# The last expert's down projection by quarters of the output columns, and the third norm's transposes by token block

## The reference

```
# 16 experts, cap = 64 tokens each, hidden width 2048
xe  = h[top_idx]                                   # (16, 64, 1024)
hid = silu(xe @ w_gate) * (xe @ w_up)              # (16, 64, 2048)
ye  = (hid @ w_down) * top_w                       # (16, 64, 1024)
x   = x + gate2 * zeros(512, 1024).at[top_idx].add(ye)
# second block
xn  = x * rsqrt(mean(x*x) + 1e-6) * g_mix          # the third norm of the kernel
z   = xn @ w_in_2 + b_in_2                         # first dense layer behind it
```

## Time and profile before

| | |
|---|---|
| median of 3 runs | 2202.88 us |
| the runs | 2198.74, 2203.45, 2202.88 us |
| the profiled execution, its own time | 2200.71 us |
| span of its records | 2198.9 us |
| mean granted clock of TensorE in it | 0.973 of full |
| PE, DVE, ACT, POOL busy | 91%, 27%, 19%, 1% of the span |
| HBM read, mean rate | 510.00 MB, 233 GB/s |

### The profile page before, as it was taken

How to read it: one execution, slowest core, us unless ns; L and a number is a source line. 1 busy time by engine, 2 the same in 40 slices (tenths; PEclk the granted TensorE clock), 3 DMA queues, 4 the chain that set the end, 5 groups by cost and what they waited for, 6 DMA issues and landing times.

```text
span 2198.9 us, 19559 instructions
## 1 busy us (share of the span) xinstructions
PE 1996.3 (91%) x8422; PEld 1112.1 (51%) x8422; DVE 602.6 (27%) x865; ACT 410.5 (19%) x617; POOL 28.3 (1%) x41
## 2 busy tenths in 40 slices
PE   3998999899968988888998889888879999999998
PEld 2555465444744434334343434343334477888887
DVE  4153437341141111010101011100126813322333
ACT  2135545500011000000000001000020213222222
POOL 0000000000000000000000000000030000000000
PEclk9999999999988999999999999999989999999999
DMA  9210033354426999999999999999972013333220
GB/s 341 77 39 20 6 110 115 120 179 141 172 96 262 415 416 416 417 417 417 415 416 416 415 416 416 416 416 417 417 254 77 20 39 115 96 96 97 96 75 39
DMA packets 143787, 513.37 MB, mean 233 GB/s; under 512 B 7891, under 2 KB 70355, under 8 KB 107731
## 3 DMA queue, kind: packets, MB, share of 16 engines
q1 hardware_dynamic: 141632, 503.35, 58.7%
q10 hardware_dynamic: 2070, 8.78, 1.0%
HBM read 510.00 MB, written 2.10 MB: 233 GB/s over the span
## 4 chain that ended last, share of the span: by engine, by line
PE 72%; DMA 18%; DVE 5%; ACT 4%; issue 1%; SPq 1%; ACTq 0%; DVEq 0%
PE ps L424 14%; DMA work<-in_w_exp_up 13%; PE ps L940 11%; PE ps L904 7%; PE ps L429 6%; PE ps L1083 5%; DMA ring<-in_w_exp_up 4%; PE ps L1042 4%; PE ps L1043 4%; PE ps L1044 4%; PE ps L862 3%; PE ps L642 3%; DMA ring<-in_ada_w 1%; PE ps L885 1%; PE ps L587 1%; PE ps L988 1%
## 5 line engine op out<-in xcount | busy, mean ns | idle before, releaser
L904 PE MATMUL ps<-work 128*64 128x512 f32 x1256 | 351.8, 595 | 41.7 <-DMA work<-in_w_exp_up 41.7
L424 PE MATMUL ps<-work,ring 128*128 128x512 f32 x784 | 345.9, 599 | 0.8 <-DVE work L1636 0.8
L904 PE MATMUL ps<-ring,work 128*64 128x512 f32 x792 | 242.8, 595 | 23.5 <-DMA ring<-in_w_exp_up 23.5
L424 PEld LDWEIGHTS ps<-work,ring 128*128 128x128 f32 x784 | 148.7, 192 | 186.7 <-issue 184.9
L904 PEld LDWEIGHTS ps<-work 128*64 128x64 f32 x1256 | 116.5, 137 | 232.4 <-issue 153.2
L1806 DVE TENSOR_TENSOR work<-work,ps 64x512 f32<-64x512 f32 x64 | 42.0, 692 | 505.1 <-ACT work L1358 504.5
L1358 ACT ACTIVATE work<-ps 64x512 f32<-64x512 f32 x64 | 32.6, 584 | 758.3 <-PE ps L904 758.3
L429 PE MATMUL ps<-ring,work 128*128 128x256 f32 x640 | 143.0, 386 | 2.5 <-DVE work L1703 1.7
L904 PEld LDWEIGHTS ps<-ring,work 128*64 128x64 f32 x792 | 80.8, 137 | 126.5 <-issue 82.4
L940 PE MATMUL ps<-work 128*64 128x512 f32 x600 | 140.6, 620 | 3.7 <-issue 3.1
L1042 PE MATMUL ps<-xh,wh 128*128 128x512 f32 x352 | 137.0, 389 | 0.0
(11 more groups left out here) (239 smaller groups left out, 1859.5 us busy)
## 6 DMA issues: line engine op xcount, KB each, us to landing
work<-in_w_exp_gate SPq DMA_DIRECT2D x80, 1024.0 KB, 23.2
work<-in_w_exp_up SPq DMA_DIRECT2D x77, 1024.0 KB, 23.5
work<-in_w_exp_down SPq DMA_DIRECT2D x75, 1024.0 KB, 20.9
ring<-in_w_exp_down SPq DMA_DIRECT2D x53, 1024.0 KB, 21.0
ring<-in_w_exp_up SPq DMA_DIRECT2D x51, 1024.0 KB, 22.4
ring<-in_w_exp_gate SPq DMA_DIRECT2D x48, 1024.0 KB, 22.5
ring<-in_w_in SPq DMA_DIRECT2D x27, 1024.0 KB, 5.5
ring<-in_ada_w SPq DMA_DIRECT2D x24, 1024.0 KB, 6.4
```

The lines of the kernel that those rows point to most:

```text
L424: i = e.matmul(bank(bk), piece(key)[:, off + k, 128 * j:128 * j + 128], rhs(k), start=(k == 0), stop=(k == (last or nk) - 1))
L904: i = e.matmul(PS[64 * gu:64 * gu + 64, fb, :], at(XET + 128 * k + 64 * z, 64), flat(key)[:, 512 * fb:512 * fb + 512], start=(k == 0), sto ...
```

## The change

Only the last expert is treated differently, and what follows it.

- The pieces of its down weights are cut another way. Piece n = 2q + half holds 256 output columns (quarter q) and 1024 rows of the hidden width (one half), as eight blocks of 128 rows: its rows in memory are 1 KB long where they were 4 KB.
- Down of the last expert is `last_down`: for each quarter q, 16 matmuls of 256 columns with a 128x64 stationary operand, all into partitions 64 to 127 of bank 4 or 5 (alternating by quarter). Each quarter is complete after two pieces.
- After the first half of quarter q, PE does `combine_quarter(q - 1)`: four matmuls of 256 columns with a 128x128 stationary operand into banks 6 and 7, with the two-deep wait as before, now on `x_fa`. The last quarter is combined behind all.
- DVE multiplies each quarter by the gate (64x256) and adds four 128x256 blocks to `X` (`add_quarter`). In the last quarter the additions are interleaved with the norm's reciprocals and scalings: addition tc+1 stands ahead of the scaling of block tc.
- ACT squares columns 0 to 767 of each token block once quarter 2 is added, adds the epsilon, and squares only the last 256 columns of a block after its last addition; the square root takes the rest as its bias.
- The transposes of the third norm go by token block for the first four feature blocks, which fill four banks; the other four feature blocks go as before.
- GpSimd waits for the two memsets behind the transposes where it waited for the last addition.

```
+def last_down():
+    e.wait_ge(s["x_hc"], 4 * NE)
+    e.wait_ge(s["x_xa"], 2 * NE)
+    for n in range(8):
+        q, half = n // 2, n % 2
+        key = ("ed", NE - 1, n)
+        e.wait_ge(*got[key])
+        if half == 0:
+            e.wait_ge(s["x_ym"], (30, 30, 31, 32)[q])
+        for k in range(8):
+            i = e.matmul(PS[64:128, 4 + q % 2, 0:256], at(HIDT + 64 * (8 * half + k), 64),
+                         piece(key, 8)[:, k, :], start=(half + k == 0), stop=(half + k == 8))
+        i.then_inc(s["x_dn"], 1)
+        if half == 0 and q > 0:
+            combine_quarter(q - 1)
+    combine_quarter(3)
+def combine_quarter(q):
+    ...
+    for tc in range(TC):
+        m = 4 * q + tc
+        if m < 2:  e.wait_ge(s["x_hc"], 4 * NE - 1 + m)
+        else:      e.wait_ge(s["x_fa"], m - 1)
+        e.matmul(bank(6 + m % 2, 256), at(OHWT + 128 * tc, 128), at(YE + 256 * q, 256),
+                 start=True, stop=True).then_inc(s["x_fb"], 1)
# PE, third norm
-turn(XS3, [0, 1, 2, 3], lambda c: normed(3, c), t3_free, s["t_pe"])
+for c in range(TC):
+    e.wait_ge(*normed(3, c))
+    for k in range(4):
+        ...
+        i = e.transpose(bank(k, 128, 128 * c), at(XS3 + 1024 * c + 128 * k, 128), ident)
+        if c == TC - 1:
+            i.then_inc(s["t_pe"], 1)
+for k in range(4, KD):
+    ...
# ACT
-rms(X, TP, st3, range(4), lambda c: None, s["r_a"])
+for c in range(TC):
+    e.wait_ge(s["x_fa"], 9 + c)
+    own(e.activation(..., at(X + 1024 * c, 768), ACT.Square, scale=1.0 / 32, accum_out=at(st3 + c, 1)))
+own(e.activation(at(st3a, 4), at(st3, 4), ACT.Identity, bias=cst("eps6")))
+for c in range(TC):
+    e.wait_ge(s["x_fa"], 13 + c)
+    own(e.activation(..., at(X + 1024 * c + 768, 256), ACT.Square, scale=1.0 / 32, accum_out=at(st3b + c, 1)))
+    e.activation(at(st3 + 4 + c, 1), at(st3b + c, 1), ACT.Sqrt, bias=at(st3a + c, 1)).then_inc(s["r_a"], 1)
# DVE
+for q in range(4):
+    e.wait_ge(s["x_dn"], 8 * (NE - 1) + 2 * q + 2)
+    e.tensor_tensor(rows(64, 128, YE + 256 * q, 256), PS[64:128, 4 + q % 2, 0:256],
+                    rows(64, 128, GATE2 + 256 * q, 256), ALU.mult).then_inc(s["x_ym"], 1)
+    if q < 3:
+        for tc in range(TC):
+            add_quarter(q, tc)
+add_quarter(3, 0)
+for c in range(TC):
+    if c + 1 < TC:
+        add_quarter(3, c + 1)
+    rms(3, X, XS3, st3, (c,), lambda c: e.wait_ge(s["x_fa"], 13 + c))
# GpSimd
-e.wait_ge(s["x_ca"], 64)
+e.wait_ge(s["pads"], 2)
```

More of the change, by code:

```diff
@@ L178 @@
     "wo_pe wo_t wo_x rt_pe rt_e rt_d "
-    "x_g x_oh x_xa x_xd x_ow x_ot x_oc x_gu x_sl x_hd x_ht x_hc x_dn x_ym x_cb x_ca "
+    "x_g x_oh x_xa x_xd x_ow x_ot x_oc x_gu x_sl x_hd x_ht x_hc x_dn x_ym x_cb x_ca x_fb x_fa "
     "pads dg i2_pe gl_sg gl_u cv_pe cv_a cv_d pw_in pw_o po_pe po_y mu_pe dv sqv vr_pe ln_a y_d y_a "
@@ L255, in build @@
         st1, st2, st3, st4, fin = small(8), small(8), small(8), small(8), small(8)
+        st3a, st3b = small(4), small(4)
         sh1, sc1, sh2, sc2 = small(8), small(8), small(8), small(8)
@@ L311, in source @@
                 return t["w_exp_gate" if kind == "eg" else "w_exp_up"][key[1], key[2] * 128:(key[2] + 1) * 128, :]
+            if kind == "ed" and key[1] == NE - 1:
+                q, half = key[2] // 2, key[2] % 2
+                return t["w_exp_down"][key[1], half * 1024:half * 1024 + 1024, q * 256:q * 256 + 256].rearrange("(k p) n -> p k n", p=128)
             if kind == "ed":
@@ L325, in rooms_of @@
                 return flat(key)
-            if kind == "ed" or (kind == "ff" and key[1] >= 22):
+            if (kind == "ed" and key[1] < NE - 1) or (kind == "ff" and key[1] >= 22):
                 return piece(key, 2)
@@ L885, in combine @@
                         e.matmul(bank(6 + dh), at(OHWT + 128 * tc, 128), at(YE + 512 * dh, 512), start=True, stop=True).then_inc(s["x_cb"], 1)
+            def combine_quarter(q):
+                if q == 0:
+                    e.wait_ge(s["x_oc"], NE // 2)
+                e.wait_ge(s["x_ym"], 31 + q)
+                for tc in range(TC):
+                    m = 4 * q + tc
+                    if m < 2:
+                        e.wait_ge(s["x_hc"], 4 * NE - 1 + m)
+                    else:
+                        e.wait_ge(s["x_fa"], m - 1)
+                    e.matmul(bank(6 + m % 2, 256), at(OHWT + 128 * tc, 128), at(YE + 256 * q, 256), start=True, stop=True).then_inc(s["x_fb"], 1)
+            def last_down():
[8 more added lines that the diff above has]
+                    for k in range(8):
+                        i = e.matmul(PS[64:128, 4 + q % 2, 0:256], at(HIDT + 64 * (8 * half + k), 64), piece(key, 8)[:, k, :],
+                                     start=(half + k == 0), stop=(half + k == 8))
+                    i.then_inc(s["x_dn"], 1)
+                    if half == 0 and q > 0:
+                        combine_quarter(q - 1)
+                combine_quarter(3)
             gather(0)
@@ L930, in _ @@
                     i.then_inc(s["x_ht"], 1)
+                if ex == NE - 1:
+                    last_down()
+                    break
                 for n in range(8):
@@ L942, in _ @@
                     i.then_inc(s["x_dn"], 1)
-            combine(NE // 2 - 1)
             def t3_free(k):
@@ L950, in t3_free @@
                     e.wait_ge(*turned_k(3, k - 4))
-            turn(XS3, [0, 1, 2, 3], lambda c: normed(3, c), t3_free, s["t_pe"])
+            for c in range(TC):
+                e.wait_ge(*normed(3, c))
+                for k in range(4):
+                    if c == 0:
+                        t3_free(k)
+                    i = e.transpose(bank(k, 128, 128 * c), at(XS3 + 1024 * c + 128 * k, 128), ident)
+                    if c == TC - 1:
+                        i.then_inc(s["t_pe"], 1)
+            for k in range(4, KD):
+                t3_free(k)
+                for c in range(TC):
+                    i = e.transpose(bank(k - 4, 128, 128 * c), at(XS3 + 1024 * c + 128 * k, 128), ident)
+                i.then_inc(s["t_pe"], 1)
             def xn_ready(k):
@@ L984, in _ @@
             e.wait_ge(s["pads"], 1)
-            e.wait_ge(s["x_ca"], 63)
+            e.wait_ge(s["x_fa"], 15)
             for k in range(31):
@@ L991, in _ @@
             pool_dense(9, 2, 5)
-            e.wait_ge(s["x_ym"], 32)
+            e.wait_ge(s["x_ym"], 33)
             for i in (3, 2, 0, 1):
@@ L1002, in _ @@
             pool_out(12, 2)
-            e.wait_ge(s["x_oc"], 8)
+            e.wait_ge(s["x_ym"], 34)
             for i in range(4):
@@ L1020, in o2_free @@
                 elif u == 5:
-                    e.wait_ge(s["x_ca"], 64)
+                    e.wait_ge(s["x_fa"], 16)
                 else:
@@ L1366, in _ @@
                     e.activation(at(HIDT + 256 * fb, 256), bank(6 + fb % 2, 256), ACT.Copy).then_inc(s["x_hc"], 1)
-            e.wait_ge(s["x_ca"], 64)
+            for c in range(TC):
+                e.wait_ge(s["x_fa"], 9 + c)
+                own(e.activation(at(XNT + 1024 * (c % 2), 768), at(X + 1024 * c, 768), ACT.Square, scale=1.0 / 32, accum_out=at(st3 + c, 1)))
+            own(e.activation(at(st3a, 4), at(st3, 4), ACT.Identity, bias=cst("eps6")))
+            for c in range(TC):
+                e.wait_ge(s["x_fa"], 13 + c)
+                own(e.activation(at(XNT + 1024 * (c % 2) + 768, 256), at(X + 1024 * c + 768, 256), ACT.Square, scale=1.0 / 32, accum_out=at(st3b + c, 1)))
+                e.activation(at(st3 + 4 + c, 1), at(st3b + c, 1), ACT.Sqrt, bias=at(st3a + c, 1)).then_inc(s["r_a"], 1)
             gf = bass.AP(t["g_final_2"].tensor, t["g_final_2"].offset, [[0, 128], [1, 1024]])
             e.dma_start(at(GATE1, 1024), gf).then_inc(s["l_gf"], 16)
-            rms(X, TP, st3, range(4), lambda c: None, s["r_a"])
             turned(3, [0, 1, 2, 3], lambda k, src: e.activation(xn(k), src, ACT.Copy, scale=vcol("gmix", k)), lambda: None)
@@ L1823, in _, with add_quarter @@
                         one_hot(p + 1)
[L1824 to L1829, removed]
+            def add_quarter(q, tc):
+                m = 4 * q + tc
+                xa = at(X + 1024 * tc + 256 * q, 256)
+                e.wait_ge(s["x_fb"], m + 1)
+                if m == 0:
+                    e.wait_ge(s["x_ca"], 56)
+                e.tensor_tensor(xa, xa, bank(6 + m % 2, 256), ALU.add).then_inc(s["x_fa"], 1)
+            for q in range(4):
+                e.wait_ge(s["x_dn"], 8 * (NE - 1) + 2 * q + 2)
+                e.tensor_tensor(rows(64, 128, YE + 256 * q, 256), PS[64:128, 4 + q % 2, 0:256], rows(64, 128, GATE2 + 256 * q, 256),
+                                ALU.mult).then_inc(s["x_ym"], 1)
+                if q < 3:
+                    for tc in range(TC):
+                        add_quarter(q, tc)
+            add_quarter(3, 0)
+            for c in range(TC):
+                if c + 1 < TC:
+                    add_quarter(3, c + 1)
+                rms(3, X, XS3, st3, (c,), lambda c: e.wait_ge(s["x_fa"], 13 + c))
```

## The result

| | before | after |
|---|---|---|
| median of 7 runs each, the same chip | 2201.62 us | 2211.61 us |
| the runs, lowest to highest | 2198.57 to 2203.45 | 2206.61 to 2213.70 |
| the profiled execution, its own time | 2200.71 us | 2208.84 us |
| its span | 2198.9 us | 2207.0 us |
| first matmul of the last down to first dense matmul | 39.49 us | 49.45 us |

The kernel became slower by half a percent: ratio 1.0046, 95% interval 1.0034 to 1.0058, or some +10 us where +11.1 was worked out. I call the last line of the table the seam; it moved by +9.96 us. Behind it nothing changed: from the first dense matmul to the end of the span it is 555.6 us before and 555.8 after, and in the ten profiled executions of this document it lies between 554.2 and 556.0.

What follows compares the result with a forecast made beforehand. PE was taken to bound the kernel, full in the last down and mostly waiting until the dense layer. +14.3 + 6.3 + 0.7 - 10.2 = +11.1 on 2200.71 gives 2211.8, stated as 2212.5 us, range 2207 to 2218.

Steps and rivals of the forecast that it cites:

- seam: First matmul of last down to first dense matmul: +14.3 + 6.3 + 0.7 - 10.2 = +11.1 us.
- down without combinations: Last expert's down: 128 unpaired records at 0.22 us plus 2.1 us for low clock, 16.04 to 30.3 us, +14.3.
- three combinations with switches: Quarters 0 to 2 combined on PE inside down: 2.1 us each, +6.3, plus six stationary-width switches at 0.12, +0.7.
- end of down to dense layer: Gate, additions, norm and transposes behind the last down matmul: 13.2 us where it was 23.45, -10.2.
- behind the seam: `i2` pieces and GpSimd's diagonals, wanted after the dense start: cost 0.
- The halves of the array: Last down: matmuls all writing partitions 64 to 127 don't run side by side, so down costs +14.3 us.
- Weights in 1 KB rows: Last expert's down pieces move at 346 GB/s for 410, last landing at 1619, wanted at 1637.6: cost 0.
- the cover: GpSimd's 19.94 us of diagonals end 21 us behind the dense start, wanted 55 us behind it: cost 0.
- the first three: Down: records overlap after all, 2199 us, 6%; clock stays half, 2243, 5%; weight loads no longer hidden, 2230, 6%.
- the fourth, pieces that land late: Down pieces in 1 KB rows at 6 us each, the last 5 us after it is wanted: 2218 us, 3%.
- The rival of the half clock: Clock stays at half while only half the array works, until the end of down: +31, 2243 us, 5%.
- the own case: The prediction's main case: +11.1 us, 2212.5, own range 2208 to 2216.5, chance 80%.

Runs made afterwards that it cites:

- The first experiment: Kernel before, with both column halves of the last expert's down writing partitions 64 to 127, the second in bank 5: 2214.46 us against 2201.55, ratio 1.0067.
- the third: Changed kernel with even row blocks of down into partitions 0 to 63, odd into 64 to 127, DVE adding both sums: 2195.88 us against 2201.55 before.
- the halves: Last expert's down by halves of the output columns, 512-column pieces, both array halves used, against the kernel before: 2196.82 us against 2201.55, ratio 0.9979.
- the early root in the changed kernel: Changed kernel with an unneeded square root on ACT ahead of the first squares, so its table loads under down: 2207.51 us in one execution.
- transposes alone: Kernel before with only the third norm's transposes by token block for the first four feature blocks: 2200.91 us against 2201.55, ratio 1.0001.
- both versions by quarters in both halves: Changed kernel with down's row blocks dealt to both array halves, without and with an early square root on ACT: 2195.88 and 2193.96 us.
- four banks: Changed kernel with the combinations of quarters 0 to 2 in banks 6, 7, 0, 1 in turn; one execution, 1.92 us per combination for 2.27.
- the halves with the early root: Down by 512-column output halves in both array halves, plus an unneeded early square root on ACT: 2195.76 us against 2201.32 before, ratio 0.9968.

## Why the prediction was right

| step | predicted | measured after |
|---|---|---|
| down without combinations | 30.3 us | 37.17 - 6.81 = 30.4 |
| three combinations with switches | 7.0 | 3 x 2.27 = 6.8 |
| end of down to dense layer | 13.2 | 12.3 |
| seam | +11.1 | +10.0 |
| behind the seam | 0 | 0.2 |

- *The halves of the array.* This step carried the sign. It rested on three starts in a timeline and a narrow matmul that cost as much as a wide one. The first experiment shows it alone, the third undoes it and turns the change into a gain. That the low clock at the start cost the same 2.1 us before and after is chance in part: both profiled executions happened to begin down at half clock, and others don't.
- *Weights in 1 KB rows.* 348 GB/s for about 410, as read from the `i2` pieces. No wait for a down piece in the chain, so at no cost, as said.
- *Combinations.* Two estimates, 0.3 for the wait and 0.24 for the switches; measured 0.35, and 0.14 left for the switches.
- *Behind down.* The term that was mis-sized, by 0.9 us: DVE's rounds took 1.2 us for 1.4, since its operations overlap at their edges, and block 3 was ready 8.2 us behind down for 8.7; the other 0.4 lies in the last transposes, 4.0 us for 4.5, where the clock came back at 1650, before their end.
- *The rivals.* Records of the new line were never side by side, the clock was full from 1606 on, and records ran at 0.22 with weight loads hidden, so the first three fell; the fourth, pieces that land late, fell with the chain that holds no DMA in down. GpSimd's matrices are built from 1652.01 on, and the convolution's matmuls come 54.94 us behind the dense start both before and after, so the cover held.
- *Two figures that don't add up.* The rival of the half clock was priced at +31 us, but its own terms (55 for 30.3, 11 for 7.0) give 28.7. The upper end of the own case, 2216.5, lies 1.4 us above 2200.71 + 14.4. Neither touches the forecast.

What the change set out to do works: quarters, the early square and the new order of the transposes together shorten what lies behind down from 23.45 to 12.3 us; how much each gives wasn't measured, save for the order. It paid for that with half of the array in the stage ahead, and with 6.8 us of combinations there.

## What to carry to other kernels

Before work is re-cut, look in the timeline at which matmuls start at the same time: a matmul with 64 stationary columns is cheap only beside a partner that writes the other half of the partitions, and a cut that needs its results in one half takes the partner away. If a sum has one output tile only, its row blocks can be dealt to both halves and added afterwards (0.9 us here behind the last quarter, for 3.5 us of matmuls saved with each quarter). When a table load stands alone behind the last dependence, a dummy operation ahead of it takes it off the path; here that gave 1.3 us, and in two of three versions TensorE's clock stayed full as well.

## What the runs showed of the hardware that I had not expected

The granted clock at the start of the last down isn't the same in every execution. It was 0.50 at the first matmul in the profiled executions of before, after, the one-half kernel, the halves and the early root in the changed kernel, and 1.00 in those of the transposes alone, both versions by quarters in both halves, and four banks; in the halves with the early root it fell a microsecond behind the first matmul. PE's instructions ahead are the same in all ten. In the five at 0.50 the clock fell among the short transposes ahead of down; what decides isn't shown. It is worth 2.1 us of this stage (48 records of 256 columns in 12.65 us against 10.57), so seams are to be compared only with their clock beside them, and so are the stretches behind down. Transposes alone brought the clock back: before, it rose at 1642 with nothing but transposes on PE since 1638.12.
